# Output product with its row work drawn in behind it, and its last two column blocks made tile by tile

## What is computed

```python
y = (hn * jax.nn.sigmoid(o)).astype(o.dtype)
yx = y @ w_out                                  # the output product, 1024x1024x1024
x = x + g1[..., None, :] * rmsnorm(yx, post_mix_g[i])
hx = modulate(rmsnorm(x, pre_ffn_g[i]), sh2, sc2)
u, g = jnp.split(hx @ up_w, 2, axis=-1)         # the up product
g = dwconv3(...)                                # along the grid's rows
yx = (jax.nn.silu(g) * u) @ down_w
x = x + g2[..., None, :] * rmsnorm(yx, post_ffn_g[i])
```

## Time and profile before

| | us |
|---|---|
| median of 3 runs | 3656.32 (3654.83 to 3665.72) |
| the profiled execution | 3656.11 |
| its span, first to last instruction | 3654.3 |
| PE busy in the span | 3260.7 (89%) |
| mean granted TensorE clock | 0.944 |

### The profile page before, as it was taken

One profiled execution on the slowest core, in us unless ns is written; L12 is line 12 of the kernel. 1 busy time (PEld: TensorE's weight loads), 2 busy tenths in 40 slices (PEclk: granted clock), 3 DMA queues, 4 the chain that ended last, 5 costly groups with the idle time before them and its releaser, 6 DMA issues.

```text
span 3654.3 us, 37088 instructions
## 1 busy us (share of the span) xinstructions
PE 3260.7 (89%) x14921; PEld 2429.9 (66%) x14942; DVE 1475.8 (40%) x2595; ACT 869.0 (24%) x1523; POOL 746.3 (20%) x322
## 2 busy tenths in 40 slices
PE   4995888888689997999999989999979499999997
PEld 2452345555676896888888854448869378888886
DVE  3007699885342236222222263113453732222226
ACT  2012344445222312111111131003431222112111
POOL 2000000000421113333333220001111523223223
PEclk9997888899799998999999999999989699999999
DMA  6101210101122011111111131100020211111112
GB/s 149 44 23 58 81 35 24 35 24 36 58 81 87 24 36 52 46 46 46 54 50 46 46 124 46 46 26 14 14 87 30 81 47 47 46 54 49 46 47 115
DMA packets 173897, 191.72 MB, mean 52 GB/s; under 512 B 24347, under 2 KB 137883, under 8 KB 173260
## 3 DMA queue, kind: packets, MB, share of 16 engines
q1 hardware_dynamic: 164560, 177.20, 15.4%
q10 hardware_dynamic: 9212, 12.79, 1.1%
HBM read 174.19 MB, written 15.78 MB: 52 GB/s over the span
## 4 chain that ended last, share of the span: by engine, by line
PE 61%; issue 16%; DVE 12%; POOL 6%; ACT 3%; DMA 1%; POOLq 0%; ACTq 0%; SPq 0%; DVEq 0%
PE psum L628 9%; PE psum L629 9%; PE psum L630 9%; PE psum L621 7%; PE psum L611 6%; POOL weights_parts L2245 3%; PE psum L1021 3%; PE psum L741 3%; DVE x_cols L1671 2%; POOL region L2297 2%; DVE rows L1669 2%; PE psum L782 2%; PE psum L1041 2%; PE psum L735 2%; DVE stats L1590 1%
## 5 line engine op out<-in xcount | busy, mean ns | idle before, releaser
L2245 POOL TENSOR_TENSOR weights_parts<-weights,weights_parts 128x2048 fp32r<-128x2048 f32 (+1 forms) x82 | 377.3, 4601 | 907.8 <-ACT weights_parts L1152 907.8
L628 PE MATMUL psum<-x_cols_parts,weights_parts 128*128 128x512 f32 x1344 | 525.5, 391 | 26.7 <-POOL weights_parts L2245 24.9
L630 PE MATMUL psum<-x_cols_parts,weights_parts 128*128 128x512 f32 x1344 | 524.5, 390 | 0.0
L630 PE MATMUL psum<-weights_parts,region_parts 128*128 128x512 f32 (+1 forms) x1120 | 409.3, 365 | 0.0
L628 PE MATMUL psum<-weights_parts,region_parts 128*128 128x512 f32 x864 | 337.3, 390 | 6.9 <-DVE region_parts L2199 5.8
L629 PE MATMUL psum<-weights_parts,region_parts 128*128 128x512 f32 x864 | 336.8, 390 | 0.0
L628 PEld LDWEIGHTS psum<-x_cols_parts,weights_parts 128*128 128x128 f32 x1344 | 253.5, 189 | 80.5 <-issue 25.9
L630 PEld LDWEIGHTS psum<-x_cols_parts,weights_parts 128*128 128x128 f32 x1344 | 253.5, 189 | 53.0
L629 PE MATMUL psum<-x_rows_parts,weights_parts 128*128 128x512 f32 x704 | 275.2, 391 | 0.0
L1152 ACT ACTIVATE weights_parts<-weights 128x2048 fp32r<-128x2048 f32 (+1 forms) x82 | 155.0, 1890 | 467.1 <-DMA region<-in_bup_h_dram 142.7
L628 PE MATMUL psum<-weights_parts,x_cols_parts 128*128 128x256 f32 x768 | 220.3, 287 | 28.4 <-POOL wide_parts L2275 12.2
(11 more groups left out here) (305 smaller groups left out, 5001.2 us busy)
## 6 DMA issues: line engine op xcount, KB each, us to landing
weights<-in_ada_w_dram SPq DMA_DIRECT2D x24, 1024.0 KB, 5.2
weights<-in_ffn_up_w_dram SPq DMA_DIRECT2D x44, 512.0 KB, 4.8
weights<-in_w_up_dram SPq DMA_DIRECT2D x16, 1024.0 KB, 5.1
weights<-in_w_down_dram SPq DMA_DIRECT2D x16, 1024.0 KB, 5.1
weights<-in_m_in_w_dram SPq DMA_DIRECT2D x7, 2048.0 KB, 7.9
weights<-in_ffn_down_w_dram SPq DMA_DIRECT2D x10, 1024.0 KB, 5.0
weights<-in_xa_wkv_dram SPq DMA_DIRECT2D x4, 2048.0 KB, 8.2
x_scratch<-x_rows SPq DMA_DIRECT2D x16, 512.0 KB, 6.6
```

Of the source, the lines that this page charges most:

```text
L628: pe.matmul(o, lhsT=a_hi, rhs=b_hi, start=(first and i == 0), stop=False)
L630: m = pe.matmul(o, lhsT=a_lo, rhs=b_hi, start=False, stop=(last and i == len(terms) - 1))
L2245: pool.tensor_tensor(WLO[buf][:, 0:width], WRAW[buf][:, 0:width], WHI[buf][:, 0:width], ALU.subtract).then_inc(s("w_lo"), 1)
```

## The change

- The output product's blocks 0 and 1 stay as they were. Blocks 2 and 3 are made together: for each row tile t first block 2's tile, then block 3's (`out_tile`), with both weight blocks resident, in the two buffers.
- Statistics of Q are taken at every 256-column copy (`copy_out` with a bn_stats) and joined per tile (`branch_stats`).
- XN now lies in Q. The second mean square is ACT's (`new_rows`: Square with a sum, then Sqrt), for tiles 0 to 5 the scaling too (`scale_rows`); DVE scales tiles 6 and 7.
- PE's 16 groups of transposes are spread (`turn_rows`): groups 0 to 3 behind tile 5, groups 4 to 7 behind tile 6, 8 to 11 behind tile 7, and 12 to 15 after the up product's first tile.
- DVE makes both parts of the columns (`split_columns`); ACT makes the high part of every second group from 8 on. POOL's 16 subtractions and the row work's second statistics on DVE are gone. X_LO2 lies in the extra buffer (first half) and in the first four tiles of XR, so only four tiles of x are stored and read back.
- The first up weights are loaded early into the region buffer (G0_RAW), split on ACT behind tile 7's work and subtracted on POOL behind the additions. The clearing of Q on POOL (`memset`) moves behind the second up weights' subtraction.

```diff
+            load_up(0, 0, G0_RAW, s("g0_in"))
+            for b in range(MO0 + 2, MO0 + 4):
+                load(b)
+
+            for t in range(NT // 2):
                 sp.wait_ge(s("x_new"), t + 1)
                 sp.dma_start(x_d[:, D * t:D * t + D], XR[:, t, :]).then_inc(s("x_out2"), 16)
...
+            for t in range(NT):
+                for j in (2, 3):
+                    if t == 0:
+                        split_weights(MO0 + j)
+                    out_tile(j, t)
+                if t in (5, 6):
+                    pe.wait_ge(s("xn_act"), 4)
+                    for i in range(4 * t - 20, 4 * t - 16):
+                        turn_rows(i)
+            pe.wait_ge(s("xn_act"), 6)
+            pe.wait_ge(s("xn_dve"), 2)
+            for i in range(8, XF_UP):
+                turn_rows(i)
+            pe.wait_ge(s("w_lo"), F2 + 1)
+            pe.wait_ge(s("xf_lo"), 8)
+            first_up2(FT["xtf"] + XF_UP, 0, 0)
+            for i in range(XF_UP, 16):
+                turn_rows(i)
+            first_up2(FT["up2"] + 1, 1, 0)
+            pe.wait_ge(s("xf_lo"), 16)
+            first_up2(FT["up2"] + 2, 0, 1)
+            first_up2(FT["up2"] + 3, 1, 1)
...
+            for t in range(NT):
+                tile_root(4, t)
+                if t >= 2:
+                    new_rows(t - 2)
+                    scale_rows(t - 2)
+                if t >= 6:
+                    for i in range(4 * t - 24, 4 * t - 20):
+                        modulated(i)
+            act.wait_ge(s("g0_in"), 48)
+            act.wait_ge(t_ready, TT["mout"] + 32)
+            act.activation(WHI[1][:, :], G0_RAW, ACT.Copy).then_inc(s("w_hi"), 1)
+            new_rows(6)
+            new_rows(7)
+            for i in range(8, XF_UP):
+                modulated(i)
...
+            for t in range(NT):
+                for j in (2, 3):
+                    copy_out(j, t)
+                branch_stats(t)
+                branch_scale(4, t)
+                if t >= 2:
+                    new_rstd(t - 2)
+                if t >= 6:
+                    for i in range(4 * t - 24, 4 * t - 20):
+                        split_columns(i)
+            new_rstd(6)
+            scale_rows(6)
+            new_rstd(7)
+            scale_rows(7)
+            dve.wait_ge(s("x_out2"), 16 * (NT // 2))
+            dve.wait_ge(s("xn_act"), 4)
+            for i in range(8, 16):
+                split_columns(i)
...
+            add_branch(0, range(NT))
+            pool.wait_ge(s("w_hi"), F2 + 1)
+            pool.tensor_tensor(WLO[1][:, :], G0_RAW, WHI[1][:, :], ALU.subtract).then_inc(s("w_lo"), 1)
...
+            low(0, F2 + 2)
+            pool.wait_ge(f_ready, FT["xtf"] + 17)
+            pool.memset(Q[:, :, :], 0.0).then_inc(s("y_zero"), 1)
...
-            pool.wait_ge(s("x_back2"), 32)
-            add_branch(1)
+            pool.wait_ge(s("x_back2"), 16)
+            add_branch(1, range(NT))
```

More of the change, by code:

```diff
@@ L327, in o_used, with out_at @@
             return max(10 + m, o_ready(h, m) + 2)
-        XN = view(R, 0, (NT, D))
+        XN = Q
+        eps_col = view(R, 15563, (1,))
+        XF_UP = 12
+        def out_at(j, t):
+            return 8 * j + t if j < 2 else 14 + 2 * t + j
+        G0_RAW = view(R, 8192, (4 * BW,))
         UU = view(R, 8192, (2, T))
@@ L397, in build_program @@
         MO0 = len(blocks)
-        fine_blocks(I["m_out_w_2"][0], t_ready, TT["mout"], 8)
+        for j in range(4):
+            fine.append(len(blocks))
+            block_of([cols_of(I["m_out_w_2"][0], HALF * j, HALF * j + HALF)], t_ready, TT["mout"] + (8 * (j + 1) if j < 2 else 32))
         G0 = len(blocks)
@@ L444, in load, with load_up @@
                     sp.dma_start(WB[b % 2][:, :, a:z], src).then_inc(w_in[b % 2], 16)
+            def load_up(g, c, raw, done):
+                for half in range(2):
+                    sp.dma_start(raw.rearrange("p (k n) -> p k n", k=KC)[:, :, P * half:P * half + P],
+                                 w_u[:, bass.ds(g * BW + (P * c + FF2 * half), P)].rearrange("(k p) n -> p k n", p=P)).then_inc(done, 16)
+                sp.dma_start(cw[:, c % 4, :], I["conv_h"][bass.ds(g * 4 + c, 1)].rearrange("a p c -> p (a c)")).then_inc(done, 16)
             for b in range(WO0):
@@ L1098, in down2 @@
                         product(PS[:, 4 + n % 4, :], terms2(t, range(n_k), c0, bufs[j])).then_inc(t_ready, 1)
-            for c in range(3):
+            for c in range(1, 3):
                 up2(0, c, 1 - c % 2, F2 + c + 1)
@@ L1510, in _, with new_rows, scale_rows, modulated @@
                 split_block(b)
[L1511 to L1520, removed]
+            def new_rows(t):
+                u = NT + t
+                act.wait_ge(s("x_new"), t + 1)
+                mark(act.activation(XN[:, t, :], XR[:, t, :], ACT.Square, accum_out=ve[:, u:u + 1]))
+                settled()
+                act.activation(sdv[:, u:u + 1], ve[:, u:u + 1], ACT.Sqrt, bias=eps_col, scale=1.0 / D).then_inc(s("x_sd"), 1)
+            def scale_rows(t):
+                act.wait_ge(s("x_rs"), t + 1)
+                act.activation(XN[:, t, :], XR[:, t, :], ACT.Copy, scale=rs[:, NT + t:NT + t + 1]).then_inc(s("xn_act"), 1)
+            def modulated(i):
+                k, n = i % KC, FT["xtf"] + (i if i < XF_UP else i + 1)
                 act.wait_ge(f_ready, n + 1)
@@ L2346, in _, with add_branch @@
                                    WI[:, i % 2, :].rearrange("p (a b) -> p a b", a=MH), ALU.mult).then_inc(s("m_qs"), 1)
-            def add_branch(i):
-                for t in range(NT):
+            def add_branch(i, tiles):
+                for t in tiles:
                     pool.wait_ge(s("b_norm"), NT * i + t + 1)
```

146 lines of the change are left out of this document (83 added, 63 removed).

## The result

The changed kernel took **3637.98 us** (median of 5 runs, 3636.09 to 3638.92), the kernel before beside it 3658.9 (5 runs, 3654.83 to 3665.72): a ratio of 0.994, with a 95% interval of 0.9926 to 0.9955. That is faster by more than the 0.3% of the prediction, 2.0 us over the forecast of 3636.0 and inside its range. Beside the experiments the kernel before ran 22 more times, with medians of 3657.21 (7 runs) and 3656.86 (15), so that some 19 us are nearer to what the change earns than the 20.9 between these two medians. The profiled execution took 3636.09 us with a span of 3634.3, 20.0 less than before in both.

The account below looks back on a forecast made before the run. PE was held by DVE's row work, then POOL's column subtractions. 2871.5 without waits plus 9.2, 4.9, 6.3, 16.4 and 3.1 of clock gave 2911.4 against 2931.8: 20 us less, 3636 us, range 3627 to 3650.

Parts of the forecast that it names:

- What bounds the kernel: Before the first up chunk's end, DVE's row work (36.70 us), then POOL's subtractions (13.56), hold PE; later code keeps the lead.
- The sum: First up chunk's last copy: 2871.5 without waits, plus four waits and clock loss, 2911.4 against 2931.8; 20 us less.
- Wait 1: PE waits behind the first tile of blocks 2 and 3 for block 3's weights, 9.2 us.
- Wait 2: Behind tile 5, PE's first transposes wait for ACT's scaling of tile 3, 4.9 us.
- Wait 3: Behind tile 6, PE waits for banks that ACT empties, 5.7 us, plus 0.6 for three further groups.
- Wait 4: Behind tile 7, PE waits for DVE's scaling of tiles 6 and 7, 16.4 us; 14.1 if POOL doesn't hold DVE.
- The transposes: PE's 16 groups ahead of the first up chunk's end: 12 at 0.6 us and 4 at 0.47, 9.1.
- The clock: PE runs at 1.2 GHz for some 3.4 us behind each of the four waits, losing 3.1 us in all.
- What was priced at nothing: The tile loop, DVE's new column subtractions and the early load of up weights, among others, cost PE 0 us.
- A: Rival: no wait for block 3's weights, or DVE not held behind tile 7; 9.2 to 11.5 more gain, 3626; chance 0.05.
- B: Rival: POOL's additions hold DVE's reciprocals, so DVE bounds the tile loop; 13 of 20 us lost, 3649; chance 0.12.
- C: Rival: PE's clock stays at 1.2 GHz between 2806 and 2911; 65 us more, 3698; chance 0.05.

Follow-up runs that it names:

- e_skew4: The changed kernel with block 2's first four tiles made by themselves, then block 3's first four, then pairs; 3629.27 us.
- e_late: The changed kernel without the early load of the first up weights, which are loaded where the kernel before had them; 3639.19 us.
- e_pipe2: The changed kernel with x's row work one tile earlier and tile 7's copies on DVE ahead of the second four column steps; 3626.42 us.
- e_skew8: The changed kernel with all eight tiles of block 2 ahead of block 3's, undoing only the tile-by-tile order; 3636.87 us.
- the best version: The changed kernel with the edits of e_pipe2 and e_skew4 together; 3616.14 us.
- e_tail: The changed kernel with ACT's roots of tiles 6 and 7 ahead of its split of the up weights; 3635.33 us (two runs).
- e_part: The kernel before with the 16 column subtractions on DVE and the first up weights split ahead of ACT's groups, product order kept; 3650.04 us.

## Why the prediction was right, and where it was off

**What bounds the kernel** held: everything behind the first up chunk kept the lead (722.8 against 722.5 us).

**The sum** by its terms: 163.1 us were forecast from the product's start (2748.4) to the copy (2911.5), 165.48 were measured. So the mechanism was right and the gain 2.4 too large in its own stretch. The absolute time of the copy fits to 0.01 only by chance, since the product began 2.3 earlier than I had it.

- *Wait 1*: 9.2 forecast, 8.71 measured; e_skew4 took all but 0.34 of it away.
- *Wait 2*: 4.9 against 4.67. *Wait 3*: 5.7 against 5.43; the 0.6 for the groups behind it didn't show as a wait. Square with its sum at 1.23 instead of 1.34 is 0.1 of each.
- *Wait 4*: 16.4 against 16.04, but by parts that erred both ways. ACT's part was shorter (four groups 2.77, not 3.2, and Square 1.23), so both roots were there at 2879.07. Unheld, DVE would have had tile 7 scaled at 2879.07 + 0.15 + 0.75 and some 0.1 of hops, about 2880.1; it was 2883.20, so **the hold cost 3.1, not 2.3**, and it fell on the last column subtraction (L2273), not on L2262, since DVE's queue was still in the first half's columns when POOL started.
- *The transposes* are the term that was mis-sized: 12 groups at 0.6 and 4 at 0.47, together 9.1. The four batches of four groups have rows of 3.67, 3.65, 3.65 and 1.91, but a row reaches over the start of the matmul behind it. From start to next start they take 3.32, 3.30, 3.30 and 1.66: **11.6**, that is 0.83 for a group at 1.2 GHz and 0.42 at 2.4. My 0.6 came from 32 transposes in a row behind one wait, in which the clock rises on the way: the first 3.3 us were at 0.50 and the 2.0 behind them at 0.99, with about 16 transposes in each. Cut into four batches of 16, three of them behind a wait, all 48 of those run cold. The range's upper end for them, 0.67 a group, was under it too.
- *The clock*: behind the waits, transposes left out, PE stayed at 1.2 GHz for another 3.0, 2.7, 0.4 and 2.2 us, and the steps of 0.21 instead of 0.12 us and 0.43 instead of 0.23 lost about 4.0 there, against 3.1.

Waits 1.9 less, transposes 2.5 more, the clock 0.9 more, and 0.9 of small things (most of it the last matmul ahead of each wait, which takes 0.28 where the sum has a step of 0.12): 2.4 over the forecast for the stretch. The 2.3 of the earlier start covered that in the profiled execution; that is luck.

**What was priced at nothing**: the tile loop was, with PE never waiting between tiles (DVE was busy for 3.6 us of each, where I had 4.7); the early load was (e_late); DVE's column subtractions weren't quite, as the 4.92 above says.

**The rivals.** A didn't come: wait 1 stood at 8.71 and DVE was held. B didn't come, but its condition was hardly met: between tiles PE had no wait, and in the loop no reciprocal of DVE ran beside an addition (L2258 ends as POOL's begins, 2840.46 + 0.15 against 2840.62); the copies and statistics that did kept their 0.41 and 0.43. Where a reciprocal did stand beside POOL, it wasn't held (e_pipe2's at 2869.00, 0.16). e_skew8 shows that another DVE step is held by an addition (1.14); with that hold and block 2's copy and statistics, 0.87 more for a tile, its 4.44 would be 5.3, still under PE's 5.76. C didn't come: 0.99 in the tile loop and the full clock back by 2849, 2862 and 2889. The rule of the Trainium skill, "TensorE: Matmul & The Clock Gate", section "A second HAM failure mode: psum-queue depth-cycling", of a clock that goes up and down with PE's pauses, agrees with the trace: behind each of the four waits PE starts at 1.2 GHz and comes back in 3.0 to 6.0 us. What it costs stays in those few us, the 4.0 and the transposes' 2.5 above.

**What stays open.** The fourth wait is still 11.7 + 2.7 in the best version. Its parts are known (ACT's roots and split, POOL's last addition and subtraction, DVE's held steps), but a version with that work moved off POOL wasn't tried. Why the product's start varies by 8.5 us between executions of the same code wasn't followed up either: between the change and before, 0.65 of the 2.34 was there by 20 us and 2.2 by 310.

## What to carry to other kernels

When row work is moved beside matmuls, list for each of the two orders what PE will wait for next: by columns it was the row work, by tiles the second block's weights, and four tiles of the one ahead of the other beat both. What is left is mostly the tail behind the last tile. There the place of a step in a queue decides who waits, and moving steps within DVE's queue only moved the time (e_pipe2); look for what holds DVE beside it, here POOL's long subtraction, though no run shows what its absence would give. And price PE's short work behind a wait at the low clock, each piece by itself, not by the mean of a long run.

## What the runs showed of the hardware

- DVE is held by POOL in more cases than I had: beside a POOL addition or subtraction a two-input subtraction took 4.92 instead of 0.69, a scaling 2.87 instead of 0.75, a cast 3.58 instead of 0.42 and a two-input step on one column 1.30 instead of 0.16. Reciprocals (0.16, beside e_pipe2's subtraction) and statistics (0.43) were not. The Trainium skill, "SBUF — State Buffer", section "SBUF: two separate sides", has the lock for a DVE instruction in a 2-port mode as well as for one with two inputs in SBUF. That the casts and scalings (512 columns in 0.42 us, 1024 in 0.75) are in such a mode is an inference, shown by no run here.
- Four groups of four fp32 transposes take 3.65 us behind a wait and 1.91 with the clock up. In the changed kernel the clock came back 3.7, 5.5 and 6.0 us behind three waits, so short work right behind such a wait ran at 1.2 GHz from its first piece to its last. In e_tail it came back within the third batch, which took 3.34. And behind the same 1.98 us of waiting ahead of the product, the granted clock was 1.00 in the kernel before and 0.50 for 3.0 us in e_part, so that two executions can differ by over 1 us with the same waits.
- The start of a stretch behind 2746 us of unchanged code varied by 8.5 us, 0.2% of the span. An effect of a few us has to be measured from a point close ahead of it.
